# Second block's first projections taken from the unnormalised residual, and ScalarE's base of a tile put ahead of the silu of the one behind it

## What is computed

```python
h = modulate(rms_norm(x, norm_g[l, 0]), shift[:, 0], scale[:, 0])
x = x + 0.5 * gate[:, 0, None, :] * swiglu(h, ffn1_w_in[l], ffn1_w_out[l])

h = modulate(rms_norm(x, norm_g[l, 1]), shift[:, 1], scale[:, 1])
x = x + gate[:, 1, None, :] * token_mixer(h, ...)

h = modulate(rms_norm(x, norm_g[l, 2]), shift[:, 2], scale[:, 2])
x = x + 0.5 * gate[:, 2, None, :] * swiglu(h, ffn2_w_in[l], ffn2_w_out[l])
```

## Time and profile before

| | us |
|---|---|
| median of 3 runs | 1982.19 |
| lowest, highest | 1977.8, 1983.47 |
| the profiled execution | 1982.89 |
| its span, first to last instruction | 1981.2 |

### The profile page before, as it was taken

The page is one execution under the profiler, slowest core; times in us unless marked ns, Lnnn a source line. Parts: engine busy times, 40 slices in busy tenths (PEclk is TensorE's granted clock), DMA queues, the critical chain, the costliest instruction groups (busy, mean ns, idle before and its releaser), DMA issues.

```text
span 1981.2 us, 25807 instructions
## 1 busy us (share of the span) xinstructions
PE 1936.3 (98%) x9544; PEld 1588.3 (80%) x9544; DVE 1008.8 (51%) x1409; ACT 738.2 (37%) x1291; POOL 191.5 (10%) x242
## 2 busy tenths in 40 slices
PE   6999999999999999999999999999999999999998
PEld 5888878766688888888887788898788888888887
DVE  6688866575454563333334666444543473333332
ACT  3345243465532342223222664343423342322332
POOL 1101110000000000000011235035000000000010
PEclk9999999999999999999999999999999999999999
DMA  8967922311043323333333232211334323333331
GB/s 301 310 176 222 316 64 88 85 33 44 23 116 113 100 86 99 92 104 90 98 88 108 75 96 80 67 46 31 87 95 126 112 81 112 95 96 93 95 97 56
DMA packets 330902, 212.87 MB, mean 107 GB/s; under 512 B 21374, under 2 KB 315451, under 8 KB 330303
## 3 DMA queue, kind: packets, MB, share of 16 engines
q1 hardware_dynamic: 319296, 170.58, 30.1%
q0 software_dynamic: 10368, 37.75, 5.4%
q10 hardware_dynamic: 1150, 3.35, 0.5%
HBM read 204.31 MB, written 7.35 MB: 107 GB/s over the span
## 4 chain that ended last, share of the span: by engine, by line
PE 91%; DVE 4%; DMA 2%; ACT 1%; issue 1%; ACTq 0%; POOL 0%; DVEq 0%; POOLq 0%
PE psum L434 26%; PE psum L436 25%; PE psum L435 25%; PE psum L1423 2%; DMA ada_w<-in_ada_w 1%; DVE ada_sum L2166 1%; PE psum L1207 1%; PE psum L1239 1%; PE psum L1220 1%; DVE delta_qkv_T L2166 1%; PE psum L1105 1%; PE psum L1121 1%; PE psum L1311 1%; PE psum L1369 1%; PE psum L957 1%
## 5 line engine op out<-in xcount | busy, mean ns | idle before, releaser
L434 PE MATMUL psum<-act_hi,w_hi 128*128 128x512 f32 x1616 | 648.9, 402 | 4.8 <-DVE act_lo L2166 2.5
L436 PE MATMUL psum<-act_hi,w_lo 128*128 128x512 f32 x1616 | 632.1, 391 | 0.0
L435 PE MATMUL psum<-act_lo,w_hi 128*128 128x512 f32 x1616 | 631.6, 391 | 0.0
L393 DVE TENSOR_TENSOR w_lo<-w_raw,w_hi 128x1024 fp32r<-128x1024 f32 x306 | 382.4, 1252 | 329.0 <-ACT w_hi L385 307.2
L385 ACT ACTIVATE w_hi<-w_raw 128x1024 fp32r<-128x1024 f32 x306 | 319.5, 1051 | 186.4 <-PE psum L436 179.0
L434 PEld LDWEIGHTS psum<-act_hi,w_hi 128*128 128x128 f32 x1616 | 304.7, 189 | 83.5 <-issue 19.6
L436 PEld LDWEIGHTS psum<-act_hi,w_lo 128*128 128x128 f32 x1616 | 304.5, 188 | 65.3
L435 PEld LDWEIGHTS psum<-act_lo,w_hi 128*128 128x128 f32 x1616 | 304.8, 189 | 61.3 <-issue 1.5
L731 POOL TENSOR_TENSOR squares<-squares 128x512 f32<-128x512 f32 x18 | 29.0, 1611 | 1254.1 <-ACT squares L1615 1254.1
L434 PE MATMUL psum<-ffn_hi,w_hi 128*128 128x512 f32 (+1 forms) x374 | 143.3, 383 | 0.0
L436 PE MATMUL psum<-ffn_hi,w_lo 128*128 128x512 f32 (+1 forms) x374 | 142.7, 382 | 0.0
(11 more groups left out here) (366 smaller groups left out, 2349.5 us busy)
## 6 DMA issues: line engine op xcount, KB each, us to landing
w_raw<-in_ffn_w_in SPq DMA_DIRECT2D x88, 512.0 KB, 3.8
ada_w<-in_ada_w POOLq DMA_DIRECT2D x72, 512.0 KB, 5.5
w_raw<-in_w_in SPq DMA_DIRECT2D x68, 512.0 KB, 4.0
w_raw<-in_mix_w_in SPq DMA_DIRECT2D x52, 512.0 KB, 3.8
w_raw<-in_ffn_w_out SPq DMA_DIRECT2D x32, 512.0 KB, 4.1
w_raw<-in_ffn_w_out SPq DMA_DIRECT2D x16, 384.0 KB, 3.4
w_raw<-in_w_branch_a SPq DMA_DIRECT2D x8, 512.0 KB, 4.0
w_raw<-in_w_out SPq DMA_DIRECT2D x8, 512.0 KB, 4.0
```

The costliest lines, as they stand in the source:

```text
L393: dve.tensor_tensor(WLO[:, n % 4, :], RAW[:, n % 4, :], WHI[:, n % 4, :].bitcast(F32), ALU.subtract).then_inc(w_lo, 1)
L434: pe.matmul(out, whi, hhi, start=start, stop=False)
L435: pe.matmul(out, whi, hlo, start=False, stop=False)
L436: return pe.matmul(out, wlo, hhi, start=False, stop=stop)
```

## The change

**Round 2 gets a raw pair.** `RAW_AT`, `AHEAD_OF` and the counts that go with them gain an entry for r = 2. ScalarE now also writes the raw high half of each residual tile during `ffn1_out`, VectorE the raw low half. The shift's share is made in four halves (`bias_half`) that all stand behind residual tile 6. TensorE runs `raw_pair(2)` on small2 and the first k chunk and then `first_pair` on k chunks 1 and 2. VectorE scales both raw tiles by `RROW` into SBUF (`STMP`, `UTMP`) and adds the shift's share to the k tile; tile 0 of the convolution reads `UTMP` instead of PSUM.

**The order of the convolution stage.** TensorE's loop starts at tile 3. The transposes of tiles 0 and 1 stand in the middle of tile 3 and behind it, that of tile 2 in the middle of tile 4, that of tile 3 behind tile 4, from where the order is as before. On ScalarE `conv_base(t)` now stands ahead of `conv_silu(t - 1)` for t = 0 to 5.

**The end.** Two of the four last sums move from behind the last matmul into the last tile, and the store of token rows 384 to 511 goes from SyncE's queue to ScalarE's.

```diff
-        RAW_AT, H_AT, AHEAD_OF = {1: 8, 3: 32}, {1: 16, 2: 24, 3: 40}, {1: "ffn1_in", 3: "ffn2_in"}
+        RAW_AT, H_AT = {1: 8, 2: 24, 3: 40}, {1: 16, 2: 32, 3: 48}
+        AHEAD_OF = {1: "ffn1_in", 2: "small2", 3: "ffn2_in"}
...
                         mm.then_inc(sem("raw_used"), 1)
-                    if kk == 1:
+                    if kk == 0 and r == 2:
+                        pe.wait_ge(sem("bias_parts"), 3)
+                        for t in range(2):
+                            for half in range(2):
+                                mm = pe.matmul(PS[:, 7, t:t + 1], BSUM2[:, 2 * t + half, :], ONES[:, 0:1],
+                                               start=(half == 0), stop=(half == 1))
+                        mm.then_inc(sem("bias_sum"), 1)
+                    elif kk == 1:
...
             ffn_out("ffn1_out")
-            rms_sum(2)
-            rms_spread(2)
-            first_pair([(Place("small2", 0), 0), (Place("k2", 0), 0)], H_AT[2])
+            raw_pair(2)
+            first_pair([(Place("k2", 0), 1), (Place("k2", 0), 2)], H_AT[2])
...
-            for t in range(1, 24):
+            for t in range(3, 24):
                 pl, k = conv_place(t)
                 quarter(pl, k, 0)
                 quarter(pl, k, 1)
+                if t <= 4:
+                    behind(2 * t - 5)
                 middle(t)
                 quarter(pl, k, 2)
                 quarter(pl, k, 3)
-                behind(t)
+                behind(2 if t == 3 else t)
...
             out_stage("ffn1_out", 2, 3)
-            root(2)
-            norm_hi(2, MOD + 24)
-            split_hi(act, Place("small2", 0), AHEAD)
...
+            before_norm(2)
+            split_hi(act, Place("k2", 0), 3)
+            act.wait_ge(sem("raw_scaled"), 2)
...
             for t in range(24):
                 pl, k = conv_place(t)
-                split_hi(act, pl, k + AHEAD)
+                if t >= 2:
+                    split_hi(act, pl, k + AHEAD)
+                if t <= 5:
+                    conv_base(t)
                 if t:
                     conv_silu(t - 1)
+                else:
+                    act.activation(SMR2[:], STMP[:], ACT.Identity, bias=col(AG)).then_inc(sem("small_rows"), 1)
                 if 0 <= t - 2 < 16:
                     lengths(t - 2)
                 small_steps(t)
-                conv_base(t)
+                if t > 5:
+                    conv_base(t)
...
+            def bias_half(q):
+
+                t, kt = q // 2, 4 * (q % 2)
+                n = Place(AHEAD_OF[2], 0).chunk + t
+                dve.wait_ge(w_loaded[n % 4], 16 * (n // 4 + 1))
+                chained(tt(BHALF[:].rearrange("p (k n) -> p k n", n=P),
+                           RAW[:, n % 4, kt * P:kt * P + 4 * P].rearrange("p (k n) -> p k n", n=P),
+                           b3(col(SHIFT_OF[2] + kt, 4), P), ALU.mult))
+                ins = dve.tensor_reduce(BSUM2[:, q, :], BHALF[:].rearrange("p (k n) -> p n k", n=P), AX, ALU.add)
+                chained(ins) if q < 3 else ins.then_inc(sem("bias_parts"), 1)
...
+                    if r == 2 and f == 6:
+                        for q in range(4):
+                            bias_half(q)
...
             rms(2, COEF, MOD + 24)
-            split_lo(dve, Place("small2", 0), AHEAD)
+            small, first = Place("small2", 0), Place("k2", 0)
+            tiles_ready(dve, first, 0)
+            cnt.mark(tt(STMP[:], RROW[:], PS[:, small.bank(0), :], ALU.mult))
+            cnt.mark(tt(UTMP[:], RROW[:], PS[:, first.bank(0), :], ALU.mult))
+            chained(tt(col(AG), col(AG), col(DTB), ALU.add))
+            dve.sem_inc(bank_free[small.bank(0)], 1)
+            dve.sem_inc(bank_free[first.bank(0)], 1)
+            chained(ts(UTMP[:], UTMP[:], col(AG + 1), None, ALU.add))
+            dve.sem_inc(sem("raw_scaled"), 1)
+            split_lo(dve, first, 3)
```

More of the change, by code:

```diff
@@ L199, in two_blocks @@
         RROW, UTMP = phase("rms_rows", 54, [T]), phase("raw_tile", 56, [T])
+        STMP = phase("raw_small", 58, [T])
+        BHALF, BSUM2 = phase("bias_half", 96, [4 * P]), phase("bias_sums2", 98, [4, P])
         QK1 = phase("mlstm_qk_T", 0, [16, T])
@@ L655, in _ @@
                 sp.dma_start(ov[:, n, :], YTOK2[:, n, :]).then_inc(stored, 16)
-            for n in (2, 3):
-                sp.wait_ge(sem("out_T_taken" if n == 2 else "final_x"), KD + 2)
-                sp.dma_start(ov[:, n, 0:D - P], YTOK2[:, n, 0:D - P]).then_inc(stored, 16)
+            sp.wait_ge(sem("out_T_taken"), KD + 2)
+            sp.dma_start(ov[:, 2, 0:D - P], YTOK2[:, 2, 0:D - P]).then_inc(stored, 16)
             sp.wait_ge(sem("out_T_taken"), KD + 3)
@@ L993, in out_back, with last_sums @@
                 mm.then_inc(sem("out_T"), 1)
[L995 to L1005, removed]
+            def last_sums(half, part):
+                if part == 0:
+                    pe.wait_ge(sem("squares_added"), 6 * 3)
+                    if half:
+                        pe.wait_ge(sem("mean_recip"), NT + 4)
+                else:
+                    pe.wait_ge(sem("squares_ready"), NT + 8 * 4 + half)
+                slot = square_slot(4, KD - 1) if part else 0
+                for n in (0, 1):
+                    tok = slice((2 * half + n) * P, (2 * half + n) * P + P)
+                    mm = pe.matmul(PS[:, 4, 2 * half + n:2 * half + n + 1], SQ[:, slot, tok], ONES[:, 0:1],
+                                   start=(part == 0 and n == 0), stop=(part == 1 and n == 1))
+                if part == 0:
+                    return
                 mm.then_inc(sem("square_sum"), 1)
@@ L1635, in last_taken @@
                 copy(YTOK2[:, 3, 0:D - P], YTOK2[:, 3, 0:D - P], scale=col(RCOL + 3)).then_inc(sem("final_x"), 1)
+                act.wait_ge(sem("final_x"), KD + 2)
+                act.dma_start(out[0, 3 * P:4 * P, 0:D - P], YTOK2[:, 3, 0:D - P]).then_inc(stored, 16)
             def out_stage(name, r, per_tile, after=None):
@@ L2683, in _ @@
             dve.wait_ge(sem("x_T"), KD + 2)
-            residual("ffn1_out", 3, MOD + 16, normed=True)
             coef(1)
+            residual("ffn1_out", 3, MOD + 16, normed=True, r=2)
             rms(2, COEF, MOD + 24)
-            split_lo(dve, Place("small2", 0), AHEAD)
+            small, first = Place("small2", 0), Place("k2", 0)
[8 more added lines that the diff above has]
+            split_lo(dve, first, 3)
             def taps(t):
@@ L2693, in taps @@
                 dve.wait_ge(sem("conv_base"), 16 + t + 1)
+                rows = PS[:, pl.bank(k), :] if t else UTMP[:]
                 for j in range(1, 4):
                     o = QKV[:, slot, j:T]
-                    chained(stt(o, PS[:, pl.bank(k), 0:T - j], col(CW2 + 24 * (3 - j) + slot), o, ALU.mult, ALU.add))
+                    chained(stt(o, rows[:, 0:T - j], col(CW2 + 24 * (3 - j) + slot), o, ALU.mult, ALU.add))
                 dve.sem_inc(sem("conv_taps"), 1)
-                dve.sem_inc(bank_free[pl.bank(k)], 1)
+                if t:
+                    dve.sem_inc(bank_free[pl.bank(k)], 1)
             def ps4(bk):
@@ L2780, in _ @@
                 pl, k = conv_place(t)
-                split_lo(dve, pl, k + AHEAD)
+                if t >= 2:
+                    split_lo(dve, pl, k + AHEAD)
                 small_parts(t)
```

37 lines of the change are left out of this document (19 added, 18 removed).

## The result

| | us |
|---|---|
| before, median of 20 runs | 1982.59 (1977.8 to 1985.0) |
| changed, median of 20 runs | 1987.4 (1980.88 to 1992.34) |
| ratio, 95% interval | 1.0027, 1.002 to 1.0034 |
| predicted | 1987.8 (1980.0 to 1991.5) |
| the profiled execution of the changed kernel, its span | 1992.34, 1990.7 |

The change costs 4.8 us. That is less than the 5.9 us (0.3%) that the prediction took as the least that can be told from no change, but with 20 executions of each kernel the interval of the ratio leaves 1 out. The profiled execution was the longest of the 20. It was 3.06 us later than the profile of before already where the changed code begins (its last matmul of `ffn1_out` starts at 1070.99, before at 1067.93), so all that follows is read as lengths of stretches, not as clock times.

A forecast was written before the change was run, and what follows sets the result against it. TensorE, busy 98% of the span, was taken as the bound. Idle and work terms +0.75, lower clock +5.1 and the end -0.2 gave +5.6 us on the median 1982.19: 1987.8 us, range 1980 to 1991.5.

The forecast's parts named there:

- raw pair in place of round 2: From the last ffn1_out matmul to the end of round 2's first pair: 20.88 us becomes 14.5, gain 6.4 us.
- tile 3's low half: Behind the raw pair, TensorE ends its second pair and waits 0.4 us for tile 3's low half.
- first wait: TensorE in the middle of tile 4, before tile 2's transpose, waits 3.0 us for a ScalarE busy throughout.
- second wait: Behind tile 4, before tile 3's transpose: base 4, table load, silu 3 and squares 2 lie bare, 3.75 us.
- third wait: Behind tile 5, before tile 4's transpose: same reason as the second wait, without the load, 2.45 us.
- the four old waits go: TensorE's four stands for the decay's values in the convolution stage disappear, removing 2.55 us.
- lower clock: Behind each of three new convolution-stage waits the granted clock falls, losing 1.7 us each: 5.1 us added.
- the end: Two last sums moved into the last tile, one last store on another queue: between 0 and -0.4, taken as -0.2 us.
- Rival (d): Raw pair doesn't run through because bias halves or `w_lo` come late, each 1 us; to 1989 us; chance 0.05.
- rival (c): TensorE stays at 1.2 GHz for two spells behind each of the two long waits: 8.5 us, 1991.2 us; chance 0.17.
- Rival (a): The convolution-stage waits come but the clock stays: 1982.7 us, or 1984.4 with one drop; chance 0.24.
- The rule weighed: ScalarE table loads: the skill page's 2.66 us per switch would add 4.2 us over four loads; forecast kept 1.28 each.

The follow-up runs named there:

- e_order: The kernel before with only ScalarE's new order for tiles 1 to 5, without the raw pair and the new end: 2004.7 us, ratio 1.0115.
- e_base3: The changed kernel with ScalarE's base ahead of silu only for tiles 0 to 3, behind silu and squares for 4 and 5: 1979.7 us, ratio 0.9986.
- e_base4: The changed kernel with the base ahead of silu only for tiles 0 to 4, tile 5's behind again: 1984.6 us, ratio 1.0012.
- e_cover: The changed kernel with the first two of the four half bias products and reductions done twice: 1989.8 us in one execution.
- e_fill: The changed kernel with 10, 14 and 8 extra unread matmuls on TensorE right ahead of the three waits: 1982.9 us, ratio 0.9998.
- e_base0: The changed kernel with each base from tile 1 on behind silu and squares, as before; the raw pair stays: 1983.2 us, ratio 1.0005.
- e_turns: e_base3 with the transposes of tiles 2 to 5 and the decay's sums and rows later on TensorE, masks to fit: 1972.7 us, ratio 0.9958.
- e_turns5: e_turns with the base ahead of silu for tiles 0 to 5, as in the changed kernel: 1974.7 us, ratio 0.996.

## Why the prediction was right, point by point

| term | predicted | measured in the profile of the changed kernel |
|---|---|---|
| raw pair in place of round 2 | -6.4 | 14.56 - 20.88 = -6.32 |
| tile 3's low half | 0.4 | 0.34 |
| transpose of tile 0 | 0.1 | 0 |
| first wait | 3.0 | 2.89 |
| second wait | 3.75 | 3.94 |
| third wait | 2.45 | 2.51 |
| the four old waits go | -2.55 | all gone |
| lower clock | 5.1 | 6.2 |
| the end | -0.2 | 0: -0.44 behind the last matmul, +0.47 in the last tile |

- **Raw pair.** Round 3 was the right model. The bias halves took 7.3 us on VectorE (1057.01 to 1064.31) against 6.9, since their reductions were 1.08 to 1.10 us, not 1.02; the cover was 0.8 instead of 1.1 us, and held. Rival (d) didn't come.
- **The 20.88 us itself** was one execution. In `e_order`, which has the same round 2, it took 21.74 us: the clock was down to 0.50 from 1070.8 on, 2.8 us behind the last matmul of `ffn1_out`; in the profile of before it fell only 5.5 us behind it. Every variant with the raw pair did 1.3 to 2.3 us better against before in its median than in its stretch (changed +4.8 against +6.7, `e_base3` -3.2 against -0.9). The old round being longer in most executions than in the profiled one would explain part of that; two traces of it are too few to show it.
- **The three waits** came where and from whom the prediction said, with at most 0.2 us of error each. The second is the worked sum: base, load, silu, squares behind the tile's end.
- **The clock** was the mis-sized term in the profiled execution. One drop each of 3.4 us was right for the first and third wait. Around the second it was 6.8 us, which is what rival (c) described, but for one wait instead of two and starting inside it, so that it cost 2.8 and not 3.4. Rival (a), no drop at all, fell. The wait doesn't decide which of the two lengths comes: around the same 3.94 us it was 6.8 us in the changed kernel and in `e_base4`, 3.4 us in `e_cover`, and one of each in `e_order`.
- **The clock, over all executions.** The profile is of the slowest of 20. Each execution has its mean granted clock on record (to 0.001, about 2 us, so only averages say something); 1 less that, times the span, is the most that the lower clock can have taken over the whole launch (waits that fall into a spell are in it). It is 16.7 us in the profile of the changed kernel but 14.0 on average of its 20 executions; before, 13.6 in the profile and 14.9 on average of the 54 executions timed with the variants; `e_fill` 9.3 on average. So the three waits' lower clock costs about 14.0 - 9.3 = 4.7 us at most on average (an estimate), near the 5.1 of the prediction, and `e_fill`'s median is 4.5 us lower. The profile of the changed kernel has more of the lower clock than its average execution, that of before less.
- **The end.** From the start of the last FFN matmul to the end of the span it is 7.83 or 7.84 us in the eight traces with the new end and 8.27 in the two with the old, 0.44 less. But the column sums that now stand inside the last tile make it longer: its last 25 FFN matmuls span 3.32 us from first start to last start in each of the eight, 2.85 in the two: 0.47 more. So the 0.44 is the four column sums that no longer stand behind the last matmul; they cost as much inside the last tile, and the moved store gave nothing that the traces show, where -0.2 was forecast.
- **Sum.** -6.32 + 9.68 - 2.55 + 6.2 = +7.0 us from the measured terms (9.68 is tile 3's low half and the three waits), against +6.7 in the stretch; the two traces differ by +6.4 us from `ffn1_out`'s end to the end of the span, and the medians by +4.8. Predicted was +5.6: 1.1 us short in the clock and 0.2 off at the end for the profiled execution. With the average of 4.7 us at most for the clock the same terms give +5.5. The mechanism and the terms of idle time are shown; that the total came to 0.8 us from the measured +4.8, and the time to 0.4 (the median of before had moved from 1982.19 to 1982.59), is more than these terms, from one execution each, can promise, and owes something to luck.
- **The rule weighed.** Behind tile 4 the load starts at 1115.69 and silu 3 at 1116.98: 1.29 us, and base, load, silu and squares follow each other without a gap up to 1118.65. The Trainium skill, page "ScalarE: Activation LUTs", section "What ACT_TABLE_LOAD costs", would have a drain with it and 2.66 us in all; the trace doesn't agree here either, and a wait of 3.94 us, of which base, silu and squares as priced in the prediction already take 2.36, has no room for it.
- **What the prediction didn't see** is what `e_base0` and `e_turns` showed: that the early base is worth 3.5 us for tiles 1 to 3 together, and that the first wait, for which I had written that "nothing but less work" on ScalarE would shorten it, goes if TensorE has other work to do. It was right of ScalarE and wrong of the kernel.

## What to carry to other kernels

Before an instruction is put ahead of others on a side engine, ask what it waits for: for a tile that is already there it starts the next engine early, for one that isn't it puts everything queued behind it at that tile's end, bare if the bound engine wants it right there. When a change gives the side engines a backlog, move the points at which the bound engine asks for their results by as much, or the gain is handed back at the first one. Count a stand of TensorE of some 1.4 us or more once as idle time and once more for the lower clock that may follow it: in the ten traces a spell began in or behind 15 of the 16 stands of 2.5 to 3.9 us between the last tile of `ffn1_out` and tile 5 of the stage, and in or behind 8 of the 10 of 1.43 us.

## What the runs showed of the hardware that I had not expected

- The lower clock came in spells of 3.4 us (in or behind waits of 1.43 to 3.94 us), of 6.8 us (around some of the waits of 3.94 us, and in round 2 before) and once of 10.2 us (round 2 of `e_order`), and of no length between. A spell can begin inside a wait, and that part of it is free.
- It doesn't always come. Behind the 2.52 us that TensorE stood before 1108.92 in `e_order` the granted clock stays at 1.00 (windows):

```profile
1108.00:1110.00 2.00, 1.08 (x7) 1.03 (x8) 1.45 (x2) 1.98 (x7) 0.00 (x0) 1.00 0.00 0
1110.00:1112.00 2.00, 2.00 (x11) 1.61 (x10) 0.58 (x1) 1.38 (x4) 0.00 (x0) 1.00 0.00 0
```

- Nor did it come behind the 1.54 us of `e_base0`, nor, in `e_turns` and `e_turns5`, behind the 1.43 us of the earlier trace rows at the stage's last transposes, which comes with a spell of 3.4 us in the other eight traces (timeline of TensorE and window of `e_turns`):

```profile
1254.56 0.66 PE L1296 MATMUL psum<-constants,delta_qkv_T 128*128 128x128 f32 x4 [1.43 <-ACT delta_qkv_T L2041]
...
1256.00:1258.00 2.00, 2.00 (x12) 1.75 (x12) 2.00 (x4) 0.00 (x0) 0.00 (x0) 1.00 0.00 0
```

- Waits of 0.58 to 0.91 us in the convolution stage never brought it (`e_fill`, `e_base3`), and 32 matmuls whose result nobody read, put into longer ones, made the kernel 4.5 us faster.
- A chain on one engine repeats to the hundredth across kernels: the wait of 3.94 us stands in five places of four kernels, the first wait is 2.89 us in three kernels and 2.87 in a fourth.
